# Moving low-part subtractions of the gated feed-forward stages from VectorE to GpSimd in a 1-core two-block sequence kernel

## The chip, the cores and the metric

The kernel runs on one core of a Trainium2 chip. The time is device microseconds of one execution of the whole program. Engines are named PE (TensorE matmul), DVE (VectorE), ACT (ScalarE), POOL (GpSimd) and SP (SyncE, which issues the loads). The banks are PSUM, every other named tile lies in SBUF.

## The reference, cut to what matters

The model is a hybrid convolution and state-space layer followed by two residual layers. Each of those two has a SwiGLU feed-forward network (FFN) before and after its mixer, so four FFNs run in all, with D_MODEL = 1024, D_FF = 2816 and 512 tokens:

```python
def _swiglu(h, w_gate, w_up, w_down):
    return (jax.nn.silu(h @ w_gate) * (h @ w_up)) @ w_down

for layer in range(DEPTH_2):                    # 2
    x = x + 0.5 * _swiglu(_rmsnorm(x, g[0]), w_gate[layer, 0], w_up[layer, 0], w_down[layer, 0])
    x = x + mixer(_rmsnorm(x, g[1]))            # conv + RWKV in layer 0, attention in layer 1
    x = x + 0.5 * _swiglu(_rmsnorm(x, g[2]), w_gate[layer, 1], w_up[layer, 1], w_down[layer, 1])
```

## The kernel before, in words

**Arithmetic.** All operands are float32. A matrix product is made of three PE products: each operand is split in a high part (an ACT copy into the fp32r type, which rounds it) and a low part (value minus high part, in fp32r too), and high×high, high×low and low×high are summed in a bank. So every weight tile costs an ACT instruction for the high part and a subtraction for the low part, on DVE for gate and up weights (`gu_lo`, L574) and on POOL for all other weights (`split_lo`, L312).

**One FFN** (`e` = 0 to 3) works on 22 column blocks of 128, in two halves (`c`) of 11. For each block `n`, gate and up products are made ("a pair"), then the gate is scaled by the inverse root of the norm (`scale`), goes through SiLU on ACT (`silu`), is multiplied with up (`gated`), and the result is split into `ffn_aH` (`high`, ACT L669) and `ffn_aL` (`low`, DVE L839). After 11 blocks the down projection of the half runs as 16 units of five or six weight tiles (`unit`, L330 to L337) with `split_hi` on ACT and `split_lo` on POOL.

**Plain and summed pairs.** The first few pairs of an FFN (4, 2, 1 and 1 of them for the four FFNs, `N_PLAIN`) are plain: 48 matmuls of 512 columns. The other 80 pairs are summed: a Strassen-like scheme with seven half-size products (`ORDER` P1, P2, P6, P5, P7, P3, P4; each 12 matmuls of 256 columns, L958, L963, L966) instead of eight. It needs sums of the weight blocks and sums of the activations:

- `gu_sums` on DVE (L546, L548, L550) makes the three sums of a pair's weights from the four loaded blocks; a tile `gu_w` has 7 blocks of 512 columns. They are split in three parts: part 0 (2 blocks, 1024 columns), part 1 (the 3 sum blocks, 1536 columns), part 2 (2 blocks, 1024 columns), by `gu_hi` on ACT (L565) and `gu_lo` on DVE (L574).
- The activation sums ("state", tiles `st_f`, `st_hi`, `st_lo`, four of each) are made once for an FFN: `state_sums_dve` (three DVE instructions for each tile, L596 to L600), `state_high_act` (L590), `state_low_dve` (L606). A further difference, "turned", takes the place of half of `hH` and `hL` once the plain pairs have used them: `turned_sum_dve` (L611), `turned_high_act` (L617), `turned_low_dve` (L624).

**Order.** Each engine runs its instructions in the order in which its function issues them, and semaphores are the only link. For a summed pair `n` DVE does, in this order: part 2 low of `n`, `scale(n-1)`, sums of `n+1`, `gated(n-1)`, part 0 low of `n+1`, `first_gate(n)` (L802), `low(n-1)`, part 1 low of `n+1`, `ups(n)` (two halves: L809 reads a bank, L811 two halves of an SBUF tile). ACT does: copy of P1, `silu(n-1)`, part 0 high of `n+1`, copy, `high(n-1)`, copy, part 1 high of `n+1`, copy, part 2 high, copy. PE may start P7, P3 and P4 only when ACT has copied an earlier product from the same bank (L661). POOL has only `split_lo` in an FFN (`ffn_pool`), so nothing while pairs run. The tile `up_t` is one buffer: `ups(n)` waits until `low(n-1)` has read it.

## Time and profile before

| | |
|---|---|
| median of 3 runs | 2451.73 us (2448.91 to 2455.95) |
| the profiled execution's own time | 2448.68 us |
| its span, first to last instruction | 2446.9 us |
| mean granted TensorE clock | 0.995 |
| four FFNs within the span, about | 474 to 833, 1165 to 1512, 1512 to 1860, 2087 to 2440 us |

In the rows further down, a line of a timeline has: start in us from the span's start, length in us, engine, line of the kernel, operation, out<-in by tile names, shapes, and in brackets how long the engine had been idle and what ended that. L12 is line 12 of the kernel. Where the kernel's own lines are moved by the change, the same function has other line numbers after it.

### The profile page before, as it was taken

Reading aid. Unit: us, or ns where it says so; the run is one execution under the profiler, and the core shown is the slowest. Engines: PE = TensorE matmul, PEld = TensorE weight load, DVE = VectorE, ACT = ScalarE, POOL = GpSimd, SP = SyncE. Lnnn points to the kernel's source line nnn. Section 1 sums busy time; section 2 is a strip of 40 time slices with the busy share of each in tenths; the row PEclk is TensorE's granted clock in tenths of the full one; section 3 lists DMA queues with packets and bytes.
Section 4 is the critical chain, followed back from the end, with each engine's and each line's share of the span. In section 5 each row is a group of like instructions: output and inputs, shape, how many; then the busy total and the mean of one; then the engine's idle time right before and its main releaser. Section 6 shows DMA issues by size and latency. Waiting matters only on the chain.

```text
span 2446.9 us, 42260 instructions
## 1 busy us (share of the span) xinstructions
PE 2379.7 (97%) x16963; PEld 2003.1 (82%) x16963; DVE 1788.0 (73%) x2391; ACT 1148.8 (47%) x1758; POOL 731.5 (30%) x438
## 2 busy tenths in 40 slices
PE   8999999989999999989999999999999999999999
PEld 6666767779899777876998998998987557898997
DVE  6999986487496589865984967965956776883871
ACT  5533353455265336344652654643644344662552
POOL 3799934300301446522003012012024212004003
PEclk9999999999999999999999999999999999999999
DMA  5222224233433432002434343342434121333332
GB/s 149 78 78 78 74 65 132 58 87 91 108 104 94 112 90 76 27 3 57 116 93 111 104 114 85 87 129 70 109 91 104 49 59 53 87 96 104 103 92 90
DMA packets 420791, 214.48 MB, mean 88 GB/s; under 512 B 17317, under 2 KB 419035, under 8 KB 420603
## 3 DMA queue, kind: packets, MB, share of 16 engines
q1 hardware_dynamic: 416523, 209.05, 31.2%
q10 hardware_dynamic: 4080, 2.83, 0.5%
q8 instruction: 130, 2.13, 0.3%
q14 instruction: 58, 0.48, 0.1%
HBM read 209.22 MB, written 2.10 MB: 86 GB/s over the span
## 4 chain that ended last, share of the span: by engine, by line
PE 81%; DVE 7%; POOL 6%; ACT 3%; issue 2%; DMA 0%; ACTq 0%; POOLq 0%; DVEq 0%
PE bank L958 11%; PE bank L966 11%; PE bank L963 11%; PE bank L337 11%; PE bank L334 11%; PE bank L330 11%; POOL w_lo L312 2%; PE bank L1826 2%; PE bank L1823 2%; PE bank L1819 2%; DVE bank L1653 1%; PE bank L3363 1%; PE bank L2711 1%; PE bank L3429 1%; DVE hL L361 1%
## 5 line engine op out<-in xcount | busy, mean ns | idle before, releaser
L312 POOL TENSOR_TENSOR w_lo<-w_raw,w_hi 128x1024 fp32r<-128x1024 f32 (+5 forms) x276 | 533.0, 1932 | 1595.7 <-ACT w_hi L304 1590.9
L304 ACT ACTIVATE w_hi<-w_raw 128x1024 fp32r<-128x1024 f32 (+5 forms) x276 | 237.7, 861 | 646.7 <-PE bank L337 484.5
L574 DVE TENSOR_TENSOR gu_w_lo<-gu_w,gu_w_hi 128x1024 fp32r<-128x1024 f32 (+1 forms) x256 | 364.5, 1426 | 61.3 <-ACT gu_w_hi L565 60.6
L565 ACT ACTIVATE gu_w_hi<-gu_w 128x1024 fp32r<-128x1024 f32 (+1 forms) x256 | 303.2, 1186 | 0.0
L661 ACT ACTIVATE tmp<-bank 128x256 f32<-128x256 f32 x320 | 121.9, 381 | 199.2 <-PE bank L966 195.3
L958 PE MATMUL bank<-hH,gu_w_hi 128*128 128x256 f32 x1280 | 206.2, 284 | 7.4 <-ACT tmp L661 7.4
L966 PE MATMUL bank<-hH,gu_w_lo 128*128 128x256 f32 x1280 | 205.0, 283 | 0.0
L963 PE MATMUL bank<-hL,gu_w_hi 128*128 128x256 f32 x1280 | 204.8, 282 | 0.0
L931 DVE TENSOR_TENSOR bank<-bank,R 128x512 f32<-128x512 f32 x64 | 44.8, 699 | 201.4 <-PE bank L337 200.5
L330 PE MATMUL bank<-ffn_aH,w_hi 128*128 128x512 f32 x704 | 185.2, 395 | 0.0
L337 PE MATMUL bank<-ffn_aH,w_lo 128*128 128x512 f32 x704 | 185.0, 395 | 0.0
L334 PE MATMUL bank<-ffn_aL,w_hi 128*128 128x512 f32 x704 | 185.0, 395 | 0.0
L958 PEld LDWEIGHTS bank<-hH,gu_w_hi 128*128 128x128 f32 x1280 | 176.8, 191 | 9.5 <-ACT tmp L661 8.0
L966 PEld LDWEIGHTS bank<-hH,gu_w_lo 128*128 128x128 f32 x1280 | 175.8, 191 | 0.0
L963 PEld LDWEIGHTS bank<-hL,gu_w_hi 128*128 128x128 f32 x1280 | 175.6, 191 | 0.0
L1653 DVE SCALAR_TENSOR_TENSOR bank<-cu,par,bank 128x512 f32<-128x512 f32 x232 | 162.6, 766 | 0.0
L958 PE MATMUL bank<-st_hi,gu_w_hi 128*128 128x256 f32 x960 | 154.0, 283 | 7.0 <-ACT tmp L661 7.0
L334 PEld LDWEIGHTS bank<-ffn_aL,w_hi 128*128 128x128 f32 x704 | 132.0, 187 | 32.3
L337 PEld LDWEIGHTS bank<-ffn_aH,w_lo 128*128 128x128 f32 x704 | 132.0, 187 | 32.3
L330 PEld LDWEIGHTS bank<-ffn_aH,w_hi 128*128 128x128 f32 x704 | 131.1, 188 | 31.1
L963 PE MATMUL bank<-st_lo,gu_w_hi 128*128 128x256 f32 x960 | 153.9, 283 | 0.0
L966 PE MATMUL bank<-st_hi,gu_w_lo 128*128 128x256 f32 x960 | 153.9, 283 | 0.0
(552 smaller groups left out, 4592.8 us busy)
## 6 DMA issues: line engine op xcount, KB each, us to landing
gu_w<-in_ffn_w_gate SPq DMA_DIRECT2D x88, 512.0 KB, 4.0
gu_w<-in_ffn_w_up SPq DMA_DIRECT2D x88, 512.0 KB, 5.3
w_raw<-in_w_in SPq DMA_DIRECT2D x48, 512.0 KB, 3.8
w_raw<-in_ffn_w_down SPq DMA_DIRECT2D x64, 384.0 KB, 3.4
w_raw<-in_ffn_w_down SPq DMA_DIRECT2D x64, 320.0 KB, 3.2
w_raw<-in_even_w_in SPq DMA_DIRECT2D x26, 512.0 KB, 3.8
w_raw<-in_w_conv_out SPq DMA_DIRECT2D x8, 512.0 KB, 3.8
w_raw<-in_w_out SPq DMA_DIRECT2D x8, 512.0 KB, 3.8
```

Source lines behind the costliest of these rows:

```text
L304: nc.scalar.activation(w_hi[u % 2][:, 0:K, :], w_raw[u % 4][:, 0:K, :], ACT.Identity).then_inc(w_hi_ready, 1)
L312: nc.gpsimd.tensor_tensor(w_lo[u % 2][:, 0:K, :], w_raw[u % 4][:, 0:K, :], w_hi[u % 2][:, 0:K, :].bitcast(F32), ALU.subtract).then_inc(w_l ...
L330: nc.tensor.matmul(out, H[:, k, :], sH[:, k0 + k, :], start=start and k == 0, stop=False)
L334: nc.tensor.matmul(out, H[:, k, :], sL[:, k0 + k, :], start=False, stop=False)
L337: ins = nc.tensor.matmul(out, L[:, k, :], sH[:, k0 + k, :], start=False, stop=stop and k == K - 1)
L565: nc.scalar.activation(gu_wh[v % 2][:, b0:b1, :, :], gu_w[v % 3][:, b0:b1, :, :], ACT.Identity).then_inc(gu_hi_ready, 1)
L574: nc.vector.tensor_tensor(gu_wl[v % 3][:, b0:b1, :, :], gu_w[v % 3][:, b0:b1, :, :], gu_wh[v % 2][:, b0:b1, :, :].bitcast(F32), ALU.subtra ...
L661: s.activation(gu_copy_to(n, name), b_[:, 0:HT], ACT.Identity).then_inc(gu_copied, 1)
L958: nc.tensor.matmul(out, H[:, block, k, :], state_hi_lo(operand, k)[0], start=name in OPENS and k == 0, stop=False, skip_group_check=True)
L963: nc.tensor.matmul(out, H[:, block, k, :], state_hi_lo(operand, k)[1], start=False, stop=False, skip_group_check=True)
L966: ins = nc.tensor.matmul(out, L[:, block, k, :], state_hi_lo(operand, k)[0], start=False, stop=k == 3, skip_group_check=True)
L1653: ins = V.scalar_tensor_tensor(x_ if k == PAD else acc, x_, w_, acc, M, A)
```

## The change

POOL takes over three kinds of subtraction in the FFNs, in a new order of its own (`ffn_pool`): the activation lows `low(n)` (all 88), the part 1 lows of each summed pair's weights (`mid_low`, 80 of 128x1536), and the state lows at the FFN's border (`state_low`: all four tiles in the first FFN, tile 3 in the others, 7 in all). DVE loses the same instructions. POOL's subtractions signal on a semaphore of their own, `lo_by_pool`, and on `a_lo`. Loads (SP) and every matmul stay as they are; PE waits on other semaphores. At the start of an FFN the order on ACT and DVE is written out anew: in the first FFN all state parts and sums come earlier and the state highs are put ahead of or between SiLU and `high`; in the third and fourth FFN, where the inverse root is computed beside the first summed pair (`rooting`), two copies and the next pair's part 0 high are issued ahead of the SiLU. The core of the diff:

```diff
             st_f.append(f_lo_map.put(f"st_f{k}", [P, 3, HT]))
         hLf = Map(hH_at + 4 * DT * T).put("hL_f", [P, DT, T])
 
+        def state_lo_wait(e, k):
+
+            if e == 0 or k == 3:
+                return lo_by_pool, k + 1 if e == 0 else 4 + e + counted(GU_UNITS * e, 0, 1)
+            return st_lo_ready, 7 * e - 3 + k + 1
+
+        def turned_lo_wait(e, k):
+            return st_lo_ready, 7 * e + k + 1
+
         def state_hi_lo(name, k):
             if name in STATE_SUMS:
...
 
         def part_no(n, part):
             return counted(n, 2, 3) + part + 1
+
+        def lo_no(n, part):
+            return counted(n, 2, 2) + (part + 1 if plain(n) else 1 + part // 2)
+
+        def mid_lo_no(n):
+            return 4 + n // GU_UNITS + counted(n + 1, 0, 1)
 
         def sum_done(n, i):
...
@@ -640,8 +656,45 @@
                         gu_load(sp, n0 + GU + i - 6)
 
         def ffn_pool(pool, e):
-            for u in range(U_F[e], U_F[e] + FFN_UNITS):
-                split_lo(pool, u)
+
+            def low(n):
+                pool.wait_ge(a_hi, n + 1)
+                nc.gpsimd.tensor_tensor(aL[:, in_half(n), :], up_t[:, :], aH[:, in_half(n), :].bitcast(F32), ALU.subtract).then_inc(a_lo, 1)
+
+            def state_low(k):
+                pool.wait_ge(st_sum, 13 * e + 3 * (k + 1))
+                pool.wait_ge(st_hi_ready, 8 * e + k + 1)
+                nc.gpsimd.tensor_tensor(st_lo[k][:, :, :], st_f[k][:, :, :], st_hi[k][:, :, :].bitcast(F32), ALU.subtract).then_inc(lo_by_pool, 1)
+
+            def mid_low(n):
+                pool.wait_ge(gu_sum, sum_done(n, 3))
+                pool.wait_ge(gu_hi_ready, part_no(n, 1))
+                nc.gpsimd.tensor_tensor(gu_wl[in_half(n) % 3][:, 2:5, :, :], gu_w[in_half(n) % 3][:, 2:5, :, :],
+                                        gu_wh[in_half(n) % 2][:, 2:5, :, :].bitcast(F32), ALU.subtract).then_inc(lo_by_pool, 1)
+
+            for k in range(3 if e == 0 else 0):
+                state_low(k)
+            for c in range(2):
+                n0 = GU_UNITS * e + GU * c
+                U = U_F[e] + FFN_HALF * c
+                for i in range(GU):
+                    n = n0 + i
+                    if c == 0 and i == (2 if e == 0 else 0):
+                        state_low(3)
+                    ahead = i + 1 < GU and not plain(n + 1)
+                    early = plain(n) or (c == 0 and plain(n - 1))
+                    if ahead and early:
+                        mid_low(n + 1)
+                    if i:
+                        low(n - 1)
+                    if ahead and not early:
+                        mid_low(n + 1)
+                split_lo(pool, U)
+                low(n0 + GU - 1)
+                for i in range(1, FFN_HALF):
+                    split_lo(pool, U + i)
+                    if i == 8 and c == 0:
+                        mid_low(n0 + GU)
 
         def ffn_act(act, e):
             s = nc.scalar
@@ -713,26 +766,24 @@
                             if plain(n + 1):
                                 gu_hi(act, n + 1, 1)
                         if e == 0 and v == 1:
-                            state_part_act(act, e, 0)
+                            for k in range(4):
+                                state_part_act(act, e, k)
                             inverse_root()
                             state_high_act(act, e, 0)
+                            state_high_act(act, e, 1)
                             silu(n - 1)
+                            state_high_act(act, e, 2)
                             high(n - 1)
-                            state_part_act(act, e, 1)
-                            state_high_act(act, e, 1)
                             continue
                         if v == 1:
                             inverse_root()
-                        if v:
-                            silu(n - 1)
+                        if e == 0 and v == 2:
+                            state_high_act(act, e, 3)
                         if not plain(n + 1):
                             gu_hi(act, n + 1, 1)
                         if v:
+                            silu(n - 1)
                             high(n - 1)
-                        if e == 0 and v == 2:
-                            for k in (2, 3):
-                                state_part_act(act, e, k)
-                                state_high_act(act, e, k)
                         if not plain(n + 1):
                             turned_high_act(act, e)
@@ -740,9 +791,16 @@
                     rooting = v == 1 and c == 0
                     if rooting:
                         inverse_root()
-                        copy(n, COPIES[2])
-                    else:
-                        copy(n, COPIES[0])
+                        copy(n, "p5")
+                        copy(n, "u3")
+                        gu_hi(act, n + 1, 0)
+                        silu(n - 1)
+                        gu_hi(act, n + 1, 1)
+                        high(n - 1)
+                        gu_hi(act, n + 1, 2)
+                        copy(n, "g2")
+                        continue
+                    copy(n, COPIES[0])
                     if v:
                         silu(n - 1)
...
@@ -834,10 +890,6 @@
                 v.wait_ge(gu_up, counted(n + 1, 0, 2))
                 V.tensor_tensor(up_t[:, :], gate_t[:, :], up_t[:, :], ALU.mult).then_inc(act_ready, 1)
 
-            def low(n):
-                v.wait_ge(a_hi, n + 1)
-                V.tensor_tensor(aL[:, in_half(n), :], up_t[:, :], aH[:, in_half(n), :].bitcast(F32), ALU.subtract).then_inc(a_lo, 1)
-
             for c in range(2):
                 n0 = GU_UNITS * e + GU * c
@@ -849,14 +901,18 @@
                         if v_ == 0 and not plain(n + 1):
                             state_sums_dve(v, e, 3)
                             gu_lo(v, n + 1, 0)
-                            state_low_dve(v, e, 3)
                             turned_sum_dve(v, e)
-                            gu_lo(v, n + 1, 1)
                             turned_low_dve(v, e)
                             continue
                         if e and v_ == 0:
                             state_sums_dve(v, e, 3)
-                            state_low_dve(v, e, 3)
+                        if e == 0 and v_ == 2:
+                            scale(n - 1)
+                            state_sums_dve(v, e, 3)
+                            gu_lo(v, n + 1, 0)
+                            gu_lo(v, n + 1, 1)
+                            gated(n - 1)
+                            continue
                         if plain(n + 1):
                             if e or v_:
                                 gu_lo(v, n + 1, 0)
@@ -867,24 +923,17 @@
                             gu_lo(v, n + 1, 0)
                         if e == 0 and v_ == 1:
                             state_sums_dve(v, e, 0)
+                            state_sums_dve(v, e, 1)
                             scale(n - 1)
-                            state_low_dve(v, e, 0)
+                            state_sums_dve(v, e, 2)
                             gated(n - 1)
-                            low(n - 1)
-                            state_sums_dve(v, e, 1)
-                            state_low_dve(v, e, 1)
                             continue
                         if v_:
                             scale(n - 1)
+                        if v_:
                             gated(n - 1)
-                            low(n - 1)
-                        if e == 0 and v_ == 2:
-                            for k in (2, 3):
-                                state_sums_dve(v, e, k)
-                                state_low_dve(v, e, k)
                         if not plain(n + 1):
                             turned_sum_dve(v, e)
-                            gu_lo(v, n + 1, 1)
                             turned_low_dve(v, e)
                         continue
                     rooting = v_ == 1 and c == 0
@@ -897,19 +946,16 @@
                         scale(n - 1)
                     if ahead and not summed and not rooting:
                         gu_sums(v, n + 1)
+                    if rooting:
+                        gu_lo(v, n + 1, 0)
                     if v_:
                         gated(n - 1)
-                    if ahead:
+                    if ahead and not rooting:
                         gu_lo(v, n + 1, 0)
                     first_gate(n)
-                    if v_:
-                        low(n - 1)
-                    if ahead:
-                        gu_lo(v, n + 1, 1)
                     ups(n)
                 scale(n0 + GU - 1)
                 gated(n0 + GU - 1)
-                low(n0 + GU - 1)
                 if c == 1 and e < 3:
                     q = norm_no["dve"]
                     norm_no["dve"] += 1
@@ -938,8 +984,7 @@
                         elif j == 3:
                             gu_lo(v, n0 + GU, 0)
                         elif j == 4:
-                            for part in range(1, len(parts(n0 + GU))):
-                                gu_lo(v, n0 + GU, part)
+                            gu_lo(v, n0 + GU, 1 if plain(n0 + GU) else 2)
                         elif j == 6:
                             gu_sums(v, n0 + GU + 1)
                 x_tile(DT - 1)
@@ -959,9 +1004,9 @@
                                  skip_group_check=True)
             for k in range(4):
                 if sums is not None:
-                    pe.wait_ge(st_lo_ready, sums + k + 1)
+                    pe.wait_ge(*(turned_lo_wait if operand == "S3" else state_lo_wait)(e, k))
                 nc.tensor.matmul(out, H[:, block, k, :], state_hi_lo(operand, k)[1], start=False, stop=False, skip_group_check=True)
-            pe.wait_ge(gu_lo_ready, part_no(n, part))
+            pe.wait_ge(*((lo_by_pool, mid_lo_no(n)) if part == 1 else (gu_lo_ready, lo_no(n, part))))
             for k in range(4):
                 ins = nc.tensor.matmul(out, L[:, block, k, :], state_hi_lo(operand, k)[0], start=False, stop=k == 3, skip_group_check=True)
             ins.then_inc(gu_done, 1)
```

(The two places where PE waits for `gu_lo_ready` by a new count in plain pairs are left out, and the semaphore's declaration.)

**What moves, on DVE.** Before, one summed pair of the steady part of a half (from `ups` of a pair to `ups` of the next) reads:

```order
L811 TENSOR_TENSOR tmp_68<-tmp_67 128x256
L574 TENSOR_TENSOR gu_w_lo_79<-gu_w_76,gu_w_hi_82 128x1024
L824 TENSOR_TENSOR tmp_64<-tmp_64,R 128x512
L546 TENSOR_TENSOR gu_w_77<-gu_w_77 128x1024
L548 TENSOR_TENSOR gu_w_77<-gu_w_77 128x512
L550 TENSOR_TENSOR gu_w_77<-gu_w_77 128x512
L835 TENSOR_TENSOR tmp_68<-tmp_64,tmp_68 128x512
L574 TENSOR_TENSOR gu_w_lo_80<-gu_w_77,gu_w_hi_83 128x1024
L802 TENSOR_TENSOR tmp_64<-bank,tmp_65 128x256
L839 TENSOR_TENSOR ffn_aL<-tmp_68,ffn_aH 128x512
```

(followed by the 128x1536 low of part 1 and L809). With the change the same place on DVE reads:

```order
L867 TENSOR_TENSOR tmp_68<-tmp_66 128x256
L590 TENSOR_TENSOR gu_w_lo_79<-gu_w_76,gu_w_hi_82 128x1024
L880 TENSOR_TENSOR tmp_64<-tmp_64,R 128x512
L562 TENSOR_TENSOR gu_w_77<-gu_w_77 128x1024
L564 TENSOR_TENSOR gu_w_77<-gu_w_77 128x512
L566 TENSOR_TENSOR gu_w_77<-gu_w_77 128x512
L891 TENSOR_TENSOR tmp_68<-tmp_64,tmp_68 128x512
L590 TENSOR_TENSOR gu_w_lo_80<-gu_w_77,gu_w_hi_83 128x1024
L858 TENSOR_TENSOR tmp_64<-bank,tmp_69 128x256
L865 TENSOR_TENSOR tmp_68<-bank,tmp_69 128x256
```

The activation low (L839) and the 128x1536 low are gone; the rest stands in the same order, with L865 directly behind L858.

**What moves, on POOL.** Between the down projections of two halves POOL had nothing; now its rows at the start of the first FFN's pairs are:

```order
L667 TENSOR_TENSOR st_lo_90<-st_f_94,st_hi_86 128x768 [waits state_hi_ready,state_sums]
L662 TENSOR_TENSOR ffn_aL<-tmp_68,ffn_aH 128x512 [waits a_hi_ready]
L667 TENSOR_TENSOR st_lo_91<-st_f_95,st_hi_87 128x768 [waits state_hi_ready,state_sums]
L662 TENSOR_TENSOR ffn_aL<-tmp_68,ffn_aH 128x512 [waits a_hi_ready]
L672 TENSOR_TENSOR gu_w_lo_80<-gu_w_77,gu_w_hi_82 128x1536 [waits gu_w_hi_ready,gu_w_sums]
```

In the steady part an activation low (L662) and a part 1 low (L672) take turns, one of each for a pair.

## Rows read from the trace of the kernel before

**Rows 1.** The page: busy time, share of the span and instructions of each engine.

```profile
PE 2379.7 (97%) x16963; PEld 2003.1 (82%) x16963; DVE 1788.0 (73%) x2391; ACT 1148.8 (47%) x1758; POOL 731.5 (30%) x438
```

**Rows 2.** Waits of PE, longest in total: us in total, times, longest us.

```profile
PE bank L958 <- ACT tmp L661: 14.4, 6, 5.6
```

**Rows 3.** PE's timeline at two entries; busy times: us, PE, PEld, DVE, ACT, POOL, clock, DMA.

```profile
533.09 1.23 PE L958 MATMUL bank<-st_hi,gu_w_hi 128*128 128x256 f32 x4 [5.61 <-ACT tmp L661]
...
1537.34 0.74 PE L958 MATMUL bank<-hH,gu_w_hi 128*128 128x256 f32 x4 [3.71 <-ACT tmp L661]
...
533.00:538.50 5.50, 5.42 (x25) 5.42 (x26) 5.43 (x8) 2.09 (x5) 0.00 (x0) 0.50 0.00 0
...
685.00:782.00 97.00, 97.00 (x786) 95.40 (x785) 80.90 (x107) 57.48 (x93) 5.27 (x3) 1.00 0.36 99
```

**Rows 4.** DVE's timeline, one summed pair of the first FFN.

```profile
543.01 1.22 DVE L574 TENSOR_TENSOR gu_w_lo<-gu_w,gu_w_hi 128x1024 fp32r<-128x1024 f32 x1
...
544.74 1.22 DVE L546 TENSOR_TENSOR gu_w<-gu_w 128x1024 f32<-128x1024 f32 x1
...
547.33 0.68 DVE L835 TENSOR_TENSOR tmp<-tmp,tmp 128x512 f32<-128x512 f32 x1
...
549.07 0.42 DVE L802 TENSOR_TENSOR tmp<-bank,tmp 128x256 f32<-128x256 f32 x1
...
549.40 0.68 DVE L839 TENSOR_TENSOR ffn_aL<-tmp,ffn_aH 128x512 fp32r<-128x512 f32 x1
...
550.45 1.76 DVE L574 TENSOR_TENSOR gu_w_lo<-gu_w,gu_w_hi 128x1536 fp32r<-128x1536 f32 x1 [0.36 <-ACT gu_w_hi L565]
...
552.46 0.42 DVE L811 TENSOR_TENSOR tmp<-tmp 128x256 f32<-128x256 f32 x1
...
552.79 1.22 DVE L574 TENSOR_TENSOR gu_w_lo<-gu_w,gu_w_hi 128x1024 fp32r<-128x1024 f32 x1
```

**Rows 5.** ACT's timeline: the same pairs, then two pairs of the second half.

```profile
548.05 0.63 ACT L669 ACTIVATE ffn_aH<-tmp 128x512 fp32r<-128x512 f32 x1 [0.48 <-DVE tmp L835]
...
548.86 1.48 ACT L565 ACTIVATE gu_w_hi<-gu_w 128x1536 fp32r<-128x1536 f32 x1
...
557.84 0.64 ACT L669 ACTIVATE ffn_aH<-tmp 128x512 fp32r<-128x512 f32 x1 [0.35 <-DVE tmp L835]
...
729.09 0.63 ACT L669 ACTIVATE ffn_aH<-tmp 128x512 fp32r<-128x512 f32 x1 [0.35 <-DVE tmp L835]
...
739.04 0.63 ACT L669 ACTIVATE ffn_aH<-tmp 128x512 fp32r<-128x512 f32 x1 [0.31 <-DVE tmp L835]
```

**Rows 6.** POOL's subtraction and products: from the chain, and from the groups by form.

```profile
119.76 2.37 POOL w_lo L312
...
L1281 POOL TENSOR_TENSOR tmp<-tmp,tmp 128x512 f32<-128x512 f32 x16 | 20.7, 1295 | 3.4 <-PE bank L1920 2.2
```

**Rows 7.** Timelines of POOL and DVE where both work at once.

```profile
634.39 1.58 POOL L312 TENSOR_TENSOR w_lo<-w_raw,w_hi 128x640 fp32r<-128x640 f32 x1 [1.55 <-ACT w_hi L304]
...
1505.39 1.57 POOL L312 TENSOR_TENSOR w_lo<-w_raw,w_hi 128x640 fp32r<-128x640 f32 x1 [1.54 <-ACT w_hi L304]
...
321.24 3.81 POOL L312 TENSOR_TENSOR w_lo<-w_raw,w_hi 128x512 fp32r<-128x512 f32 x1 [4.30 <-ACT w_hi L304]
...
634.25 0.69 DVE L933 SCALAR_TENSOR_TENSOR xT<-bank,xT 128x512 f32<-128x512 f32 x1
...
634.97 2.08 DVE L574 TENSOR_TENSOR gu_w_lo<-gu_w,gu_w_hi 128x1024 fp32r<-128x1024 f32 x1
...
1505.04 0.48 DVE L596 SCALAR_TENSOR_TENSOR st_f<-xT,par,st_f 128x256 f32<-128x256 f32 x1
...
1505.56 1.69 DVE L598 SCALAR_TENSOR_TENSOR st_f<-xT,par,st_f 128x256 f32<-128x256 f32 x1
```

**Rows 8.** DVE's timeline at the entry of the third FFN.

```profile
1524.72 1.22 DVE L611 TENSOR_TENSOR hL_f<-xT 128x1024 f32<-128x1024 f32 x1
...
1527.52 1.67 DVE L624 SCALAR_TENSOR_TENSOR hL<-hL_f,par,hH 128x256 fp32r<-128x256 f32 x4
```

More of the change, by code:

```diff
@@ L446, in build @@
         st_lo_ready = sem("state_lo_ready")
+        lo_by_pool = sem("border_state_lo_then_gu_mid_lo_ready_by_gpsimd")
         STATE_SUMS = ("S1", "N2", "S4")
@@ L752, in ffn_act @@
                         split_hi(act, U)
-                    if not rooting:
-                        copy(n, COPIES[1])
+                    copy(n, COPIES[1])
                     if v:
                         high(n - 1)
-                    if not rooting:
-                        copy(n, COPIES[2])
+                    copy(n, COPIES[2])
                     if ahead:
@@ L1023, in plain_front @@
                 for which, block in ((0, 0), (1, 5)):
-                    pe.wait_ge(gu_lo_ready, part_no(n, which))
+                    pe.wait_ge(gu_lo_ready, lo_no(n, which))
                     for k in range(4):
```

## The prediction, as put on record

> **What bounds the kernel now.** I read the page first, for busy shares: PE is busy 97% of the span, POOL 30%, DVE 73% [rows 1]. A change that only moves DVE work can win no more than PE's idle time where that work is late, so the next view is PE's waits. The one large item is 14.4 us in 6 waits for a copy by ACT [rows 2]. PE's timeline places them at the start of the FFNs' summed pairs: 5.61 us in the first FFN, 3.71 us in the third, and the like in the fourth, which leaves 1.4 for the other three [rows 2, 3]. Behind the longest wait the clock is granted at 0.50 (1.2 GHz): 25 matmuls take 5.42 us, 0.217 each, against 97.00/786 = 0.123 us at full clock [rows 3], so 25 x 0.094 = 2.3 us more. All that the entries can give back is 14.4 + 2.3, plus a little for the third and fourth FFN: **some 18 us, 0.7%.**
>
> The steady pairs are the other place. There POOL gets its new work, 80 pairs long. Is there slack? DVE's timeline of one pair: the part 2 low starts at 543.01 and again at 552.79, a period of 9.78 us in which the only idle time is 0.36 us, waiting for ACT's part 1 high [rows 4]. ACT's high of the activations starts at 548.05 and 557.84: 9.79 us. In the second halves it is 729.09 to 739.04: 9.95 [rows 5]. PE is busy all of that time (97.00 of 97.00) [rows 3]. So PE and a DVE-ACT loop both fit with almost nothing over: whatever lengthens the loop is paid at once.
>
> **What POOL and DVE do to each other.** The question is what happens when POOL subtracts while DVE works. The timelines answer it. POOL runs 634.39 to 635.97. DVE's 1024-column low starts in that time, at 634.97, and takes 2.08 us instead of 1.22 [rows 4, 7]: it ends 1.08 us behind POOL's end, as if its data phase had begun there. A 256-column instruction that takes 0.48 alone takes 1.69 beside a POOL subtraction that ends at 1506.96; it ends at 1507.25, 0.29 behind [rows 7]. An instruction that reads a bank and one SBUF tile (L933, 634.25) keeps its 0.69 [rows 7]. And it works the other way: POOL's 512-column low takes 3.81 us at 321.24 instead of about 1.3 [rows 6, 7], in a run of DVE instructions. So two-SBUF-input DVE instructions and POOL's tensor_tensor take turns, and the later one stands still. **This rule, not DVE's busy time, decides the change.** The Trainium skill says the same in "SBUF — State Buffer", section "Who interferes with whom": a DVE instruction with two SBUF inputs contends with a GpSimd instruction that reads SBUF, and who starts first holds the shared port for the whole instruction. It speaks against this change. Held from POOL's start to its end, it would forbid the overlap of DVE's 0.13 us lead-in that the rows show, and add about 80 x 0.13 = 10 us to my sum; the row decides.
>
> **The steady pair, step by step.** POOL's cost: 512 columns 1.295, 1024 columns 2.37 [rows 6]; 1.075 for 512 more, so 1536 columns about **3.45 us** (DVE: 1.76 [rows 4]). It waits for ACT's part 1 high of `n+1`. Just then DVE waits for PE and does L865, which reads a bank; POOL gets the port. DVE's next is L867, two SBUF inputs, and it stands until POOL ends. It can't be passed: behind it stand the part 2 low, `scale`, the sums and `gated(n-1)`, and on that wait ACT's next high and, in ACT's order, the next part 1 high. The loop, from high to high:
> - high start to end of part 1 high: 548.05 to 550.34 = 2.29 [rows 5], and 0.11 to the subtraction's start [rows 4];
> - part 1 low on POOL: 3.45;
> - L867 ends 0.29 behind it, the next starts 0.09 before that (552.46 + 0.42 against 552.79) [rows 4, 7]: 0.20;
> - part 2 low to the next high: 543.01 to 548.05 = 5.04 [rows 4, 5].
>
> Sum **11.09 us** against 9.79, +1.30, or +1.14 against 9.95. The activation low (1.3 on POOL, 0.68 on DVE before) falls in DVE's wait for PE behind L858 and costs nothing; were that cover gone, it would block 1.2 us more.
>
> **Count.** A half of 11 pairs holds about 9 such loops (the last has no pair to prepare), four second halves 36 x 1.14 = 41.0. First halves: 7 summed pairs, 5 loops, 5 x 1.30 = 6.5; 9 pairs, 7 x 1.30 = 9.1; twice 10 pairs, 16 x 1.14 = 18.2. Together 74.8. At the end of each half no part 1 low follows and PE's backlog of ready work lets about half a loop's excess be made up: 8 x 0.7 = -5.6.
>
> **Entries.** First FFN: the 5.61 wait and the 2.3 of clock go (-7.9). The four state lows (between 1.295 and 2.37, about 1.85 each) hold the port against twelve state sums of 0.48 (0.51 apart), and `gated` of the second plain pair now stands behind them and two weight lows, which keeps two banks from the fourth pair: bounds 0 and 6 us, I take 3.4, since three of the four lows fall on DVE work. Net -4.5. Second FFN: no wait worth the name before; a 3.45 us hold beside turned sum and lows (1.22 and 1.67 [rows 8]) can cost 0 to 3.4; I take +1.8. Third and fourth: the 3.71 wait can vanish if only the copies ahead of the SiLU matter, but state low and part 1 low together hold the port 5.3 us just where DVE's turned sum and lows are due for P7; at worst +4.7. I take +2.5 each. Entries +2.3. SP's loads, the down units and the mixers keep their order; the one part 1 low moved in front of a `split_lo` in the down projection is covered by POOL's idle time there, a few tenths if not.
>
> Total 74.8 - 5.6 + 2.3 = **+71.5 us on the profiled execution's 2448.7: 2520 us.** The median of the runs shown is 3.0 above that execution, within their spread, so I leave 2520.
>
> **Rivals.**
> - *Full hiding, faster* (chance 0.05). If POOL's work and DVE's did not exclude each other in this loop, DVE would be 1.67 + 0.6 us lighter in a pair, the period would stay PE's 9.8 to 9.95, and the entries' waits would go: 2448.7 - 17 = about 2432. It decides from the point at which L867 loses less than 0.1 us to POOL. Rows 7 speak against it. No change within 0.3%, from entries lost and pairs unharmed: 0.02.
> - *A partly filled loop* (0.13). If DVE gets L867 and the part 2 low in before POOL takes the port (a DVE run keeps it, as at 321.24 [rows 7]), only the sum of port times counts: DVE's two-SBUF data (eight instructions, 2 x 1.22 for lows, 1.22 + 2 x 0.69 for sums, 2 x 0.69, 0.42, less 8 x 0.15 of lead-in: about 5.6) plus POOL's 3.45 + 1.3 - 0.3 = 4.5 is 10.1 to 10.6 a pair: +0.2 to +0.7 for some 64 loops, 2465 to 2492.
> - *Both POOL instructions block* (0.10). If the activation low isn't covered but falls on the part 0 low, each loop gains another 1.2: 74.8 + 77, about 2595.
> - *The forecast* (0.70 for 2500 to 2545, the bounds of the entries and 0.2 us either way on each of 64 loops).
>
> A measurement of this kernel can tell 0.3% (7.4 us) from no change. Faster 0.05, same 0.02, slower 0.93. For 8 in 10 the range is 2482 to 2560: it takes in the forecast's own bounds and part of the second and third rival.
>
> **What would show it.** In the changed kernel's trace: POOL's 1536-column low of 3.4 to 3.5 us; L867 at 2.5 to 3.3 us instead of 0.42, starting inside it; ACT's highs 11.0 to 11.2 us apart; PE waiting about 0.8 and 0.3 us once in each pair for ACT's copy, 60 to 80 times; the 5.6 us wait of the first FFN gone; clock near 1.00, since each gap is short. I am wrong if L867 stays near 0.42 or the period stays below 10 us.

## The result, and the profile after

The changed kernel takes **2531.78 us** (median of 4 runs, 2528.08 to 2534.72). The kernel before took 2450.76 beside it: ratio 1.0321, 95% interval 1.0309 to 1.0334, slower by 3.2%. The profiled execution has a span of 2529.6 us, 82.7 more than the 2446.9 of the one before. The forecast was 2520, in a range of 2482 to 2560: the direction and the mechanism held, and the size was 12 us short.

The page of the changed kernel, busy time and three of the costliest groups (against [rows 1]):

```profile
PE 2423.1 (96%) x16963; PEld 2015.4 (80%) x16963; DVE 1797.1 (71%) x2216; ACT 1135.4 (45%) x1758; POOL 1164.7 (46%) x613
...
L662 POOL TENSOR_TENSOR ffn_aL<-tmp,ffn_aH 128x512 fp32r<-128x512 f32 x88 | 133.4, 1516 | 452.1 <-ACT ffn_aH L722 452.1
L672 POOL TENSOR_TENSOR gu_w_lo<-gu_w,gu_w_hi 128x1536 fp32r<-128x1536 f32 x80 | 282.8, 3535 | 105.5 <-ACT gu_w_hi L581 105.5
...
L867 DVE TENSOR_TENSOR tmp<-tmp 128x256 f32<-128x256 f32 x80 | 215.6, 2695 | 0.0
```

DVE has 175 instructions fewer and is busy 9 us longer. The reason is L867, the second half of the up sum: it takes 2695 ns in the mean, where a free one takes 416. The profile counts an instruction that stands still as busy, which is why no view of waits names this loss at its source.

Waits of PE in the changed kernel (us in total, times, longest us), against [rows 2]:

```profile
PE bank L1003 <- ACT tmp L714: 44.6, 66, 3.6
...
PE bank L1011 <- POOL gu_w_lo L672: 4.5, 4, 1.9
```

Six waits for ACT's copies have become 66, one in nearly every summed pair. One summed pair of the first FFN, ACT's highs, then POOL, DVE and PE:

```profile
558.38 0.63 ACT L722 ACTIVATE ffn_aH<-tmp 128x512 fp32r<-128x512 f32 x1 [1.34 <-DVE tmp L891]
...
559.18 1.48 ACT L581 ACTIVATE gu_w_hi<-gu_w 128x1536 fp32r<-128x1536 f32 x1
...
569.55 0.63 ACT L722 ACTIVATE ffn_aH<-tmp 128x512 fp32r<-128x512 f32 x1 [1.33 <-DVE tmp L891]
```

```profile
559.08 1.56 POOL L662 TENSOR_TENSOR ffn_aL<-tmp,ffn_aH 128x512 fp32r<-128x512 f32 x1 [5.95 <-ACT ffn_aH L722]
560.80 3.51 POOL L672 TENSOR_TENSOR gu_w_lo<-gu_w,gu_w_hi 128x1536 fp32r<-128x1536 f32 x1 [0.15 <-ACT gu_w_hi L581]
```

```profile
559.39 0.42 DVE L858 TENSOR_TENSOR tmp<-bank,tmp 128x256 f32<-128x256 f32 x1
561.06 0.42 DVE L865 TENSOR_TENSOR tmp<-bank,tmp 128x256 f32<-128x256 f32 x1 [1.24 <-PE bank L1011]
561.40 3.19 DVE L867 TENSOR_TENSOR tmp<-tmp 128x256 f32<-128x256 f32 x1
564.51 1.21 DVE L590 TENSOR_TENSOR gu_w_lo<-gu_w,gu_w_hi 128x1024 fp32r<-128x1024 f32 x1
```

```profile
570.51 0.74 PE L1003 MATMUL bank<-st_hi,gu_w_hi 128*128 128x256 f32 x4 [0.57 <-ACT tmp L714]
```

From high to high it is 11.17 us (569.55 - 558.38), and it is between 11.16 and 11.19 in every steady summed pair of all eight halves. (The last two intervals of a half are shorter: 9.52 and 7.41, against 9.52 and 8.01 before.) L865, which reads a bank, runs inside POOL's subtraction at its usual 0.42; L867, which reads SBUF twice, starts inside it and ends at 564.59, 0.28 after POOL. So do 68 of the 80; the other 12 meet no part 1 low and take 0.42.

Where the 82.7 us arose, from the starts of ACT's highs of the activations in both traces; "forecast" is the prediction's terms summed over the same stretch:

| stretch | before | after | grown by | forecast |
|---|---|---|---|---|
| start to last high of FFN 1 | 776.50 | 790.57 | 14.07 | 10.9 |
| to first high of FFN 2 | 408.16 | 412.52 | 4.36 | 0 |
| to last high of FFN 2 | 268.49 | 288.76 | 20.27 | 19.8 |
| to last high of FFN 3 | 350.89 | 372.79 | 21.90 | 20.5 |
| to the end | 642.9 | 665.0 | 22.1 | 20.5 |

### The profile page after: what moved, and what is told of

It is laid out like the page before. It is cut to its first block, busy times and chain, and to the rows that moved or that the text cites. A ratio compares the mean times of both kernels' runs of the same rounds, so it can differ in the third digit from the quotient of the medians.

```text
span 2529.6 us, 42260 instructions
## 1 busy us (share of the span) xinstructions
PE 2423.1 (96%) x16963; PEld 2015.4 (80%) x16963; DVE 1797.1 (71%) x2216; ACT 1135.4 (45%) x1758; POOL 1164.7 (46%) x613
## 4 chain that ended last, share of the span: by engine, by line
PE 77%; DVE 9%; POOL 7%; ACT 3%; issue 3%; DMA 0%; ACTq 0%; POOLq 0%; DVEq 0%
PE bank L1003 11%; PE bank L334 10%; PE bank L337 10%; PE bank L330 10%; PE bank L1011 9%; PE bank L1008 9%; POOL w_lo L312 2%; PE bank L1868 2%; PE bank L1871 2%; PE bank L1864 2%; DVE bank L1698 1%; POOL gu_w_lo L672 1%; ACT tmp L714 1%; PE bank L3408 1%; DVE gu_w_lo L590 1%
## 5 line engine op out<-in xcount | busy, mean ns | idle before, releaser
L662 POOL TENSOR_TENSOR ffn_aL<-tmp,ffn_aH 128x512 fp32r<-128x512 f32 x88 | 133.4, 1516 | 452.1 <-ACT ffn_aH L722 452.1
L672 POOL TENSOR_TENSOR gu_w_lo<-gu_w,gu_w_hi 128x1536 fp32r<-128x1536 f32 x80 | 282.8, 3535 | 105.5 <-ACT gu_w_hi L581 105.5
L590 DVE TENSOR_TENSOR gu_w_lo<-gu_w,gu_w_hi 128x1024 fp32r<-128x1024 f32 x176 | 226.0, 1285 | 14.6 <-ACT gu_w_hi L581 14.0
L1003 PE MATMUL bank<-hH,gu_w_hi 128*128 128x256 f32 x1280 | 216.7, 291 | 11.1 <-ACT tmp L714 11.1
L867 DVE TENSOR_TENSOR tmp<-tmp 128x256 f32<-128x256 f32 x80 | 215.6, 2695 | 0.0
L1003 PE MATMUL bank<-st_hi,gu_w_hi 128*128 128x256 f32 x960 | 161.8, 291 | 33.6 <-ACT tmp L714 33.5
L1003 PEld LDWEIGHTS bank<-st_hi,gu_w_hi 128*128 128x128 f32 x960 | 131.8, 192 | 47.6 <-ACT tmp L714 47.5
```

The source lines that it names most:

```text
L590: nc.vector.tensor_tensor(gu_wl[v % 3][:, b0:b1, :, :], gu_w[v % 3][:, b0:b1, :, :], gu_wh[v % 2][:, b0:b1, :, :].bitcast(F32), ALU.subtra ...
L672: nc.gpsimd.tensor_tensor(gu_wl[in_half(n) % 3][:, 2:5, :, :], gu_w[in_half(n) % 3][:, 2:5, :, :], gu_wh[in_half(n) % 2][:, 2:5, :, :].bit ...
L867: V.tensor_tensor(up_t[:, HT:T], gu_copy_to(n, "u3"), gu_copy_to(n, "p5"), ALU.add).then_inc(gu_up, 1)
L1003: nc.tensor.matmul(out, H[:, block, k, :], state_hi_lo(operand, k)[0], start=name in OPENS and k == 0, stop=False, skip_group_check=True)
```

## The experiments

**e1_mid_on_dve: part 1's lows back on DVE, the rest of the change kept.**

```diff
-                    if ahead and early:
-                        mid_low(n + 1)
...
                     first_gate(n)
+                    if ahead:
+                        gu_lo(v, n + 1, 1)
                     ups(n)
```

> The changed kernel with one part undone: the 128x1536 lows of part 1 are on DVE again, at their old place ahead of the up sums; activation lows, state lows and the new orders stay as changed. Theory (port turns decide, through the 1536-column low in the loop): the period from ACT's high to the next returns to 9.8 to 10.0 us, the second half of the up sum to 0.42 us, and the whole time to 2440 to 2452 us, a little under the kernel before, since only the entries differ. Rival A (POOL's activation low in the loop is what costs, since up_t waits for it): the period stays near 11 and the time above 2500. Rival B (the new orders at the entries cost most of the 81 us): above 2480.

2447.41 us against 2453.33 before, ratio 0.9971 (0.9958 to 0.9983). The highs are 9.77 and 9.95 us apart again, and the second half of the up sum takes 0.42 us again:

```profile
558.23 0.42 DVE L859 TENSOR_TENSOR tmp<-tmp 128x256 f32<-128x256 f32 x1
```

So the whole loss hangs on the 1536-column lows. What is left of the change is worth a little. The stretch with the first FFN's entry, first in the kernel before, then here (us, busy of PE, PEld, DVE, ACT, POOL, clock, DMA):

```profile
497.00:545.00 48.00, 42.39 (x223) 36.87 (x222) 39.05 (x54) 26.36 (x40) 0.00 (x0) 0.93 0.32 88
```

```profile
497.00:545.00 48.00, 45.73 (x263) 39.47 (x263) 44.92 (x50) 30.19 (x46) 15.85 (x9) 1.00 0.41 110
```

PE does 40 matmuls more in the same 48 us, at a granted clock of 1.00 instead of 0.93; the last high of that half starts 4.35 us earlier (600.90 against 605.25). From the FFN's first gate and up matmul to its last high it is 5.48 us less (295.19 against 300.67): the stage ahead had ended 1.1 us later in this profile (476.96 against 475.83). The other three FFNs, counted so, are within 0.3 us of before; in the third and fourth the waits only moved.

**e2_only_mid_on_pool: the kernel before, with nothing changed but part 1's lows on POOL.**

```diff
+            def mid_low(n):
...
-                    if ahead:
-                        gu_lo(v, n + 1, 1)
                     ups(n)
```

> The kernel before with one part of the change: only the 128x1536 lows of part 1 go to POOL; activation lows, state lows and all orders stay as before. Theory: the steady period is 11.1 to 11.2 us as in the changed kernel, since the activation low had cost nothing there, and the time 2525 to 2545, as much as or a little more than the changed kernel, because the first entry keeps its wait. Rival A (activation low): period back below 10.3 and time below 2470. Rival B (orders): time below 2480.

2536.5 us, 4.7 above the changed kernel. (e2 to e5 were each executed once; kernels executed more often spread by up to 8 us, little beside e2's, e3's and e5's differences of 60 to 170 us; e4 is read by its periods.) Two groups, then PE's wait and its longest instance:

```profile
L650 POOL TENSOR_TENSOR gu_w_lo<-gu_w,gu_w_hi 128x1536 fp32r<-128x1536 f32 x80 | 282.0, 3525 | 692.5 <-ACT gu_w_hi L569 692.5
...
L828 DVE TENSOR_TENSOR tmp<-tmp 128x256 f32<-128x256 f32 x80 | 228.4, 2854 | 0.0
```

```profile
PE bank L970 <- ACT tmp L678: 53.0, 68, 8.5
...
535.13 1.22 PE L970 MATMUL bank<-st_hi,gu_w_hi 128*128 128x256 f32 x4 [8.48 <-ACT tmp L678]
```

The period is 11.17 with DVE doing the activation lows as before, so those, moved to POOL, cost and bring nothing in the steady pairs: their cover holds, as forecast. The first FFN's wait, 5.61 before [rows 3], is 8.48 here; the new order at the entry removes it.

**e3_idle_subtractions and e4_idle_memsets: the kernel before, with POOL work in 68 of the summed pairs that nobody needs or waits for.** The first has three subtractions of 512 columns a pair, the second seven memsets of 512 columns.

```diff
+                        pool.wait_ge(gu_hi_ready, part_no(n, 1))
+                        for r in range(3):
+                            pool.wait_ge(idle_pool, idle_sent[0])
...
+                            nc.gpsimd.tensor_tensor(spare[:, :], xT[:, 0, :], xT[:, 1, :], ALU.subtract).then_inc(idle_pool, 1)
```

> The kernel before, unchanged, and beside each steady summed pair three extra POOL subtractions of 512 columns from SBUF to SBUF, started by the same part 1 high; nobody waits for their result. Theory (turns at a port): DVE is held although no semaphore links it to POOL; the 1536-column low on DVE takes turns with the 1.3 us pieces and the period grows by 2 to 3 us, to 11.8 to 12.8, the time to 2560 to 2620. Rival C (no port; the change costs because PE's low parts come late from the slower engine): nobody waits for this work, so the period stays 9.8 to 10.0 and the time 2446 to 2456.

> The same as with the idle subtractions, but the extra POOL work beside each pair is seven memsets of 512 columns (about 0.5 us each by the kernel's own memsets, 3.6 us in all), which write SBUF and read nothing. If only POOL's reads and DVE's second SBUF input take turns, the period stays 9.8 to 10.0 us and the time 2446 to 2456. If any POOL work holds DVE, it grows as with the subtractions, by 2 us or more a pair.

The subtractions: 2625.63 us, 6 above the range expected, and 12.76 a pair, inside it. The memsets: 2454.15 us, 9.77 to 10.00 a pair, as before. POOL's and DVE's timelines with the subtractions:

```profile
553.17 5.49 POOL L655 TENSOR_TENSOR spare<-xT 128x512 f32<-128x512 f32 x3 [7.26 <-ACT gu_w_hi L568]
```

```profile
553.19 2.88 DVE L577 TENSOR_TENSOR gu_w_lo<-gu_w,gu_w_hi 128x1536 fp32r<-128x1536 f32 x1 [0.35 <-ACT gu_w_hi L568]
556.00 0.41 DVE L823 TENSOR_TENSOR tmp<-bank,tmp 128x256 f32<-128x256 f32 x1
556.33 1.18 DVE L825 TENSOR_TENSOR tmp<-tmp 128x256 f32<-128x256 f32 x1
557.43 2.31 DVE L577 TENSOR_TENSOR gu_w_lo<-gu_w,gu_w_hi 128x1024 fp32r<-128x1024 f32 x1
```

and with the memsets, POOL and then DVE in the same place of a pair:

```profile
559.48 4.03 POOL L655 MEMSET spare<- 128x512 f32 x7 [5.74 <-ACT gu_w_hi L568]
```

```profile
559.52 1.76 DVE L577 TENSOR_TENSOR gu_w_lo<-gu_w,gu_w_hi 128x1536 fp32r<-128x1536 f32 x1 [0.35 <-ACT gu_w_hi L568]
561.20 0.42 DVE L823 TENSOR_TENSOR tmp<-bank,tmp 128x256 f32<-128x256 f32 x1
561.53 0.42 DVE L825 TENSOR_TENSOR tmp<-tmp 128x256 f32<-128x256 f32 x1
```

The lows of parts 1 and 2 and the second up half grow by 0.8 to 1.1 us beside the subtractions, the bank reader not at all; beside memsets nothing grows. 4 us of POOL's writing in a pair cost nothing that shows, and no other engine waits for a semaphore of this work: what costs is POOL reading SBUF while DVE wants two SBUF operands. It is the same loss as the change's with neither a product nor a signal of POOL's that anybody needs.

**e5_bank_read: the changed kernel, with one operand of L867 in a bank.**

```diff
-                V.tensor_tensor(up_t[:, HT:T], gu_copy_to(n, "u3"), gu_copy_to(n, "p5"), ALU.add).then_inc(gu_up, 1)
+                V.tensor_tensor(up_t[:, HT:T], gu_bank(n, 2)[:, 0:HT], gu_copy_to(n, "p5"), ALU.add).then_inc(gu_up, 1)
```

> The changed kernel with one operand moved: the second half of the up sum reads a PSUM bank and one SBUF copy instead of two SBUF copies (part of the computation is changed: the bank holds P3's product where the sum wants the copied one). Theory of the turns (a DVE instruction with both operands in SBUF and a POOL tensor_tensor never run together): the second half now runs inside the POOL low in 0.42 to 0.6 us instead of 3.2, and what waits is the next instruction with two SBUF operands, the low of part 2, at about 3.8 to 4.1 us instead of 1.2. DVE gains only what it could do meanwhile, so that a pair comes out at about 10.8 us instead of 11.17 and the kernel at about 2510 us (2500 to 2520). Rival A (POOL's long reading slows whatever DVE runs): the second half stays at 2.5 to 3.3 us, the period at 11.17 and the kernel at 2530. Rival B (that one wait is the whole loss, the rest of DVE's order would fit): the low of part 2 stays at 1.2 us, the period falls to 9.8 to 10.0 and the kernel to 2450.

2516.09 us, 10.83 a pair, both as expected. This kernel's result is a wrong one, so its times alone count. DVE, beside POOL's low that runs from 560.76 to 564.26:

```profile
561.03 0.42 DVE L865 TENSOR_TENSOR tmp<-bank,tmp 128x256 f32<-128x256 f32 x1 [1.25 <-PE bank L1011]
561.37 0.41 DVE L867 TENSOR_TENSOR tmp<-bank,tmp 128x256 f32<-128x256 f32 x1
561.94 3.40 DVE L590 TENSOR_TENSOR gu_w_lo<-gu_w,gu_w_hi 128x1024 fp32r<-128x1024 f32 x1 [0.16 <-ACT gu_w_hi L581]
```

The block sits on whichever instruction is the first to read SBUF twice. It moved from L867 to the low of part 2 and DVE kept only the 0.34 us that it could do in the meantime: 11.17 - 10.83. That low takes 3.40, less than the 3.8 to 4.1 expected; it ends 1.08 after POOL, as the 1024-column low of [rows 7] did.

**e6_split_part: POOL makes 512 of part 1's 1536 columns, DVE 1024.**

```diff
-                nc.gpsimd.tensor_tensor(gu_wl[in_half(n) % 3][:, 2:5, :, :], gu_w[in_half(n) % 3][:, 2:5, :, :],
+                nc.gpsimd.tensor_tensor(gu_wl[in_half(n) % 3][:, 4:5, :, :], gu_w[in_half(n) % 3][:, 4:5, :, :],
...
```

> The changed kernel with part 1 divided: GpSimd makes 512 of its 1536 columns (block 4), VectorE the other 1024, where it made all of part 1 before the change. Theory of the turns: the price of GpSimd's low is its length while it holds the reading, and that is now about 1.3 to 1.4 us instead of 3.5; DVE gives up 1.3 us of waiting and saves about 0.45 to 0.5 us of its own subtraction, so a pair lasts about 10.0 to 10.1 us and the kernel about 2452 to 2458 us: no gain over the kernel before, and some 75 us better than the changed kernel. Rival A (the loss is in the handing over, one semaphore and one place in the order for each low of GpSimd, whatever its size): the period stays above 10.8 and the kernel above 2510. Rival B (a short GpSimd low fits into the time in which DVE reads banks or is idle, so that the saved 0.5 us counts in full): a pair at 9.4 to 9.6 us and the kernel at 2425 to 2435.

2456.75 us against 2452.85, ratio 1.0019 (1.0009 to 1.0028), 10.01 a pair. DVE, then POOL:

```profile
557.73 1.23 DVE L592 TENSOR_TENSOR gu_w_lo<-gu_w,gu_w_hi 128x1024 fp32r<-128x1024 f32 x1 [0.95 <-ACT gu_w_hi L581]
558.88 0.42 DVE L867 TENSOR_TENSOR tmp<-bank,tmp 128x256 f32<-128x256 f32 x1
559.21 1.19 DVE L869 TENSOR_TENSOR tmp<-tmp 128x256 f32<-128x256 f32 x1
```

```profile
557.77 2.34 POOL L674 TENSOR_TENSOR gu_w_lo<-gu_w,gu_w_hi 128x512 fp32r<-128x512 f32 x1 [0.17 <-ACT gu_w_hi L581]
```

Both want the same high. DVE starts 0.04 us earlier and goes first, POOL takes 2.34 instead of 1.3, and then L869 stands still for 0.77 us. DVE's own low is only 0.53 shorter (1.23 against 1.76), so a pair loses 0.24, and 0.05 in the second halves, where PE had set 9.96. The time is as expected, but the 1.3 to 1.4 us of POOL's low behind it is not what came. This split is no gain either: POOL takes longer over its columns than DVE saves.

**e7_lows_on_dve, e8_old_root_order, e9_mid_again, e10_old_root_again: what of the change is worth keeping.** All are e1's kernel; e7 moves the activation lows back to DVE as well, e8 and e10 put the order at the third and fourth FFN's root back, e9 is e1 again beside e10.

```diff
-                        copy(n, "p5")
-                        copy(n, "u3")
-                        gu_hi(act, n + 1, 0)
-                        silu(n - 1)
...
+                        copy(n, COPIES[2])
+                    else:
+                        copy(n, COPIES[0])
```

> The version of e1_mid_on_dve (part 1's lows on VectorE) with the activation lows on VectorE as well, so that GpSimd keeps only 7 lows of border states and the lows of the down projection's weights. Theory of the turns: GpSimd's 512-column low holds the reading about 1.5 us a unit and VectorE's own costs about 0.55 us a unit, but TensorE, which sets the pace, sees neither as long as VectorE has more than that to spare; so the time is that of e1_mid_on_dve within 3 us (2445 to 2450), and VectorE's other instructions in units without a sum lose their waits. Rival: the activation lows of GpSimd delay VectorE on the path to TensorE in the loop as the 1536-column lows did, and with 88 of them gone the kernel gains 5 us or more (below 2442). Second rival: VectorE's order has no room for 0.55 us more in a pair, and the periods of the pairs grow by as much: 2465 or more.

> The version of e1_mid_on_dve with the order at the inverse root in the later FFNs (ScalarE's copies and SiLU, VectorE's first low) put back as it was before the change; the first FFN keeps the new order. If the gain of e1_mid_on_dve over the kernel before comes from the first FFN alone, as its trace has it (about 4 us there, the later FFNs' waits only moved), this one has the same time within 2 us (2446 to 2449). Rival: the new order at the later roots gives 2 to 3 us each and something else takes it, then this one is 2451 to 2455.

> The kernel of e1_mid_on_dve again, now beside the one of e8_old_root_order on the same chip, since the two were 1.6 us apart in different calls and the intervals of their ratios overlap. If the new order at the later roots is worth something, this one is 1.5 us or more below e10_old_root_again, as the first runs had it; if the gain over the kernel before comes from the first FFN alone, the two are within 1 us, both at 2446 to 2450.

> The kernel of e8_old_root_order again, for the comparison with e9_mid_again: within 1 us of it if the later roots' order is worth nothing, 1.5 us or more above it if it is.

| kernel | us | ratio to before, 95% |
|---|---|---|
| e1, new orders, POOL: activation and state lows | 2447.41 | 0.9971 (0.9958 to 0.9983) |
| e9, the same again | 2446.68 | 0.9971 (0.9960 to 0.9981) |
| e7, POOL: state lows only | 2447.02 | 0.9977 (0.9968 to 0.9986) |
| e8, old order at the later roots | 2449.05 | 0.9986 (0.9977 to 0.9996) |
| e10, the same again | 2447.57 | 0.9978 (0.9969 to 0.9987) |

e9 and e10, side by side, are 0.9 us apart, inside the 1 us expected if the later roots' order is worth nothing; something under 1 us can't be told. Which engine makes the activation lows makes no difference that these runs can tell either. The gain is the first FFN's entry: over the first FFN, counted from its first gate and up matmul, e1, e8, e9 and e10 all take 295.2 us and e7 295.5, against 300.7 before. Whether the state lows on POOL or the new order there bring it, no run separates. e1's kernel is the fastest found, **0.3% below the kernel before**, just at the limit of what a measurement tells.

**e11_low_first and e12_split_low_first: POOL's order in the first summed pair.** The table of stretches shows a surplus in the first FFN. Its first summed pair takes 13.32 us. DVE, POOL and PE of the changed kernel there:

```profile
541.49 0.42 DVE L865 TENSOR_TENSOR tmp<-bank,tmp 128x256 f32<-128x256 f32 x1 [6.17 <-POOL ffn_aL L662]
```

```profile
536.60 3.50 POOL L672 TENSOR_TENSOR gu_w_lo<-gu_w,gu_w_hi 128x1536 fp32r<-128x1536 f32 x1 [9.40 <-ACT gu_w_hi L581]
540.06 1.29 POOL L662 TENSOR_TENSOR ffn_aL<-tmp,ffn_aH 128x512 fp32r<-128x512 f32 x1
```

```profile
545.92 0.80 PE L1003 MATMUL bank<-hH,gu_w_hi 128*128 128x256 f32 x4 [2.13 <-ACT tmp L714]
```

L865 overwrites `up_t`, which POOL's activation low still reads. That low was ready to run since 534.5 but stands behind the part 1 low in POOL's order, though POOL was idle for 9.40 us before.

```diff
-                    early = plain(n) or (c == 0 and plain(n - 1))
+                    early = plain(n)
```

> The changed kernel with GpSimd's order altered in one pair of each FFN, the first summed one: the activation low of the pair before it now stands ahead of the part 1 low for the next pair, as it does in all later pairs. In the changed kernel's trace VectorE's first half of the up sum (it overwrites what the activation low reads) waits there 6.17 us for GpSimd's activation low, which stands behind the 3.5 us of the part 1 low while GpSimd was idle before it; the highs are 13.32 and 13.03 us apart there. If this wait was a second loss beside the steady pairs': those two periods fall to 11.3 to 11.8, some 3.5 us less for the first two FFNs; in the third and fourth ScalarE makes both highs at nearly the same time, so that one GpSimd low must wait for the other in either order, and PE's wait only moves (from 3.6 to about 2.1 behind it and 2.1 ahead of it): 2526 to 2530 in all, steady periods 11.17 as before. Rival: VectorE would be held by the part 1 low anyway (it reads two SBUF operands one instruction later), and nothing changes: 2530 to 2533, periods 13.0 to 13.3.

> The same alteration of GpSimd's order in the version of e6_split_part (GpSimd makes 512 of part 1's 1536 columns), whose trace has one period of 11.87 us in each of the first two FFNs against 10.0 in the steady pairs. Theory: these two fall to about 10.1, and the kernel to about 2453, level with the kernel before (ratio 0.999 to 1.001), as the steady pairs still cost 10.0 against 9.8 to 9.95. Rival: the entries hide it and the ratio stays at 1.002.

e11: 2525.99 us, ratio 1.0295 (1.0277 to 1.0312). The periods of 13.32 and 13.03 are 11.16 and 11.18 now, 2.16 and 1.85 less, since L865 waits for PE alone:

```profile
536.02 0.42 DVE L865 TENSOR_TENSOR tmp<-bank,tmp 128x256 f32<-128x256 f32 x1 [1.24 <-PE bank L1011]
536.36 3.18 DVE L867 TENSOR_TENSOR tmp<-tmp 128x256 f32<-128x256 f32 x1
```

In the third FFN nothing was won (last high to last high 372.63 against 372.79), as expected: PE's wait of 3.60 us became one of 2.05 for POOL's low and one of 0.26, where 2.1 and 2.1 were expected. The median fell by 5.8 where 3.5 was expected, measured at another time; the traces show 4.0 for the two pairs and 5.0 between the spans, and which of the rest is the order's stays open. e12, the same on top of e6: 2450.81 us, ratio 0.9987 (0.9978 to 0.9997), a little better than the 0.999 to 1.001 expected, with the two periods of 11.87 at 10.01 and 10.00. e1's kernel at 0.9971 is still ahead by the medians, though the intervals touch. With this wait gone and only 512 columns on POOL, the change comes out level with or just ahead of before.

## Why the prediction was right, point by point

- **Taking turns decides the change: right, and now shown.** Put back one kind of POOL instruction and the 3.2% are gone (e1); add that one alone and they come (e2); idle reads of SBUF cost, idle writes don't (e3, e4); the standstill follows the operands, not the instruction (e5).
- **The steady pair, 11.09: right but 0.08 short.** Measured by the same steps: high to end of the part 1 high 2.28 (2.29), to POOL's start 0.14 (0.11), POOL's low 3.51 (3.45), hand-over 0.20 (0.20), part 2 low to the next high 564.51 to 569.55 = 5.04 (5.04). Over 64 loops the 0.08 is 5.1 us, the largest true error. In the first halves of the first two FFNs it doesn't show, since the later pairs there stood at 9.95 before and not at the 9.79 that I took: without L865's wait, told below, the five loops of the first cost 6.4 us, forecast 6.5.
- **The ends of the halves, -5.6: right in size.** The last high-to-high interval of each half is 0.6 shorter than before, eight times, together -4.8. That PE's backlog makes this up, as the prediction has it, was not tested.
- **The lock's extent.** L867 was issued inside POOL's instruction and ended 0.28 after it, as in [rows 7], 0.14 less than its 0.42 alone. The Trainium skill, "SBUF — State Buffer", section "Who interferes with whom", says of DVE's two-port modes that whoever issues first gets the shared pair for the whole instruction. Taken over to two SBUF inputs, as the prediction did, this would make it 0.42 behind and the pair 11.3; 11.17 speaks against that. The rows don't tell whether DVE's lead-in overlapped or POOL's last read lies before its recorded end. Two other statements of that section of the Trainium skill, that a DVE instruction with one SBUF input doesn't contend and that a GpSimd instruction that only writes doesn't, agree with 0.42 and 0.41 in e5 and with e4's unchanged 9.77.
- **The activation low is covered: right** (e2 and the changed kernel share the period), and with it the rival at 2595 fell. The rival of a filled loop fell with periods of 11.16 to 11.19; that of full hiding with L867's 3.19.
- **Entries, +2.3: right in sum but for one wait.** The table's first stretches also hold stages that vary from run to run, so count each FFN from its first gate and up matmul to its last high: it grows by 13.2, 20.8, 21.9 and 22.2 us (300.67 to 313.88, 287.62 to 308.46, 292.02 to 313.93, 292.33 to 314.50). Take the loops' 0.08 away: the first FFN is 1.2 above the forecast, the second 0.2 below, the third and fourth 0.1 and 0.3 above. The first one's long wait and the half clock did go, and `gated` of the second plain pair did come late, as I had named it: PE, which had no wait there before (first row), stands 1.75 us until `gated` (second row) frees its bank.

```profile
513.28 2.10 PE L1014 MATMUL bank<-hH,gu_w_hi 128*128 128x512 f32 x8
...
515.04 0.68 DVE L888 TENSOR_TENSOR tmp<-tmp,bank 128x512 f32<-128x512 f32 x1
...
515.93 2.10 PE L1059 MATMUL bank<-hH,gu_w_hi 128*128 128x512 f32 x8 [1.75 <-issue]
```

  With this, e1 still gains 5.48 in the first FFN, where my net was 4.5. What I put at nothing is L865 behind POOL's activation low, one queue further. The step that failed is the one on what is queued on POOL in the first summed pair; e11 puts 2.2 us on it there, and 1.85 in the second FFN. There my 1.8 came out by luck: it was meant for a hold beside the turned sum and lows, and without this wait nothing of it would be left.
- **The mixer, 0 forecast, +4.36 in the table: not from the change.** No instruction differs there. From the last high of the first FFN to the first gate and up matmul of the second it is 389.04 us in the kernel before, 392.82 in the changed one, and 390.41 to 394.77 in the other twelve: 394.50 with e4's memsets and 390.41 with e3's subtractions, which lie outside it. The same way from the second FFN to the third, without a mixer, takes 58.86 or 58.87 us in all of them. The kernel before was profiled at the low end. Why the mixer varies wasn't looked into; the medians, 81.0 apart, average over it only in part.
- **The whole miss** between the two profiles, 82.7 against 71.5, is then 5.1 for the loops, 4.6 outside the FFNs (0.86 ahead of the first, 3.78 between the first two) and the 1.4 left within them.
- **PE's waits "of 0.8 and 0.3 once in each pair": half right.** 66 times, but each pair shows one wait, of 0.57. The rest of the 1.3 us lies in matmuls around it that are listed as longer (0.74 for four instead of 0.64) and in gaps too short to be listed. Time that PE loses is to be read from the period, not from the sum of its waits: 44.6 us stand there for some 80 lost.

## What to carry to other kernels

Before work goes from DVE to POOL to relieve DVE, ask what each side reads. In these runs a POOL subtraction from SBUF held up the DVE instructions with two SBUF operands that came behind it (L867: 3.19 instead of 0.42), and it took twice DVE's time for the same columns. So in this loop without slack the offload costs POOL's time, less the time that DVE no longer needs for the same work, less what DVE can do meanwhile with banks: 3.51 - 1.76 - 0.34 = 1.41 against a measured 1.39, and in e5, with two bank readers, 3.50 - 1.76 - 0.68 = 1.06 against 1.06. Look for the bill in a DVE group whose mean grew, since it appears as busy time and not as a wait. And when a buffer's last reader moves to another engine, follow that engine's queue up to the next writer of the buffer.

## What was not expected of the hardware

- Idle POOL subtractions that were added cost more than the useful one that was moved. e3's three of 512 columns, 3.9 us when alone (1295 each [rows 6]) and 5.49 there, lengthen a pair by 2.98 us; that is what three DVE instructions stand still there, 1.12 + 0.76 + 1.09. The useful 1536 columns, 3.51 us, lengthen it by 1.39: they stop one instruction for 2.77, but some 1.4 of it comes back, since DVE no longer has their 1.76 us to do.
- Who goes first changes within 0.04 us (e6: DVE at 557.73, POOL at 557.77) and decides who stands still: POOL's 512 columns took 2.34 us there, 1.3 elsewhere. Once each in the third and fourth FFN POOL's 1536 columns took 4.44 and 4.46 us instead of 3.51, beside a run of DVE work.
